# MLP of a hybrid decoder layer: one of seven products added from PSUM by VectorE in place of a ScalarE copy and a GpSimd add

## What is computed

```python
def finish_layer(x, attn_o, pool_z, ga, gp, w_attn_up, w_pool_up, w_out,
                 g_post_mix, g_pre_mlp, g_post_mlp, w_mlp_up, w_mlp_down):
...
    h = x + rms_norm(m @ w_out, g_post_mix)
    f = jnp.square(jax.nn.relu(rms_norm(h, g_pre_mlp) @ w_mlp_up)) @ w_mlp_down
    return h + rms_norm(f, g_post_mlp)
```

## Time and profile before

| | |
|---|---|
| time, median of 3 runs | 1331.14 us (1331.07 to 1332.55) |
| the profiled execution's own time | 1330.84 us |
| its span, first to last instruction | 1329.1 us |
| the 14 blocks | from about 596 to 1226 us of the span |
| busy in the span: TensorE | 1308.5 us, 98% |
| VectorE | 695.9 us, 52% |
| ScalarE | 567.4 us, 43% |
| GpSimd | 452.5 us, 34% |

### The profile page before, as it was taken

The page is one execution under the profiler, slowest core; times in us unless marked ns, Lnnn a source line. Parts: engine busy times, 40 slices in busy tenths (PEclk is TensorE's granted clock), DMA queues, the critical chain, the costliest instruction groups (busy, mean ns, idle before and its releaser), DMA issues.

```text
span 1329.1 us, 20370 instructions
## 1 busy us (share of the span) xinstructions
PE 1308.5 (98%) x7483; PEld 1205.4 (91%) x7483; DVE 695.9 (52%) x1070; ACT 567.4 (43%) x1063; POOL 452.5 (34%) x541
## 2 busy tenths in 40 slices
PE   7999999999999999999999999999999999999998
PEld 6988889999999998888989998999899989998986
DVE  6478752322222235546666566656665666566256
ACT  6355543211111144336445544554455445444432
POOL 4001584000000000103465457545754575457010
PEclk9999999999999999999999999999999999999999
DMA  8200001011111114421110111011101100110152
GB/s 256 97 33 34 17 33 38 32 48 48 48 48 34 47 57 178 146 84 60 64 64 0 63 63 55 8 63 63 46 17 63 63 35 28 63 63 32 64 189 96
DMA packets 23638, 84.42 MB, mean 64 GB/s; under 512 B 3202, under 2 KB 3282, under 8 KB 23562
## 3 DMA queue, kind: packets, MB, share of 16 engines
q1 hardware_dynamic: 17970, 64.30, 13.6%
q0 software_dynamic: 5472, 19.12, 4.4%
q10 hardware_dynamic: 144, 0.26, 0.1%
HBM read 74.38 MB, written 10.39 MB: 64 GB/s over the span
## 4 chain that ended last, share of the span: by engine, by line
PE 92%; DVE 3%; ACT 3%; issue 1%; DMA 0%; DVEq 0%; SPq 0%; ACTq 0%
PE ps L1858 20%; PE ps L1496 18%; PE ps L1497 18%; PE ps L1498 18%; PE ps L1738 9%; PE ps L1517 2%; PE ps L1891 2%; ACT pr L755 1%; DVE pr L1138 1%; PE ps L1746 1%; PE ps L1712 1%; ACT pt L775 0%; DVE pt L1185 0%; PE ps L1537 0%; PE ps L1808 0%
## 5 line engine op out<-in xcount | busy, mean ns | idle before, releaser
L1496 PE MATMUL ps<-xn,wr 128*128 128x384 f32 (+1 forms) x1384 | 455.4, 329 | 2.6 <-issue 1.5
L1497 PE MATMUL ps<-xn,wr 128*128 128x384 f32 (+1 forms) x1384 | 452.6, 327 | 0.0
L1498 PE MATMUL ps<-xn,wr 128*128 128x384 f32 (+1 forms) x1384 | 452.4, 327 | 0.0
L1496 PEld LDWEIGHTS ps<-xn,wr 128*128 128x128 f32 x1384 | 260.2, 188 | 6.7 <-issue 2.3
L1497 PEld LDWEIGHTS ps<-xn,wr 128*128 128x128 f32 x1384 | 260.3, 188 | 0.5
L1498 PEld LDWEIGHTS ps<-xn,wr 128*128 128x128 f32 x1384 | 260.1, 188 | 0.0
L618 POOL TENSOR_TENSOR acc<-acc,tmp 128x512 f32<-128x512 f32 x160 | 239.5, 1519 | 46.6 <-ACT tmp L938 44.7
L1362 DVE TENSOR_TENSOR acc<-acc,ps 128x512 f32<-128x512 f32 x216 | 143.3, 684 | 37.8 <-PE ps L1858 31.3
L938 ACT ACTIVATE tmp<-ps 128x512 f32<-128x512 f32 x168 | 97.2, 597 | 150.8 <-PE ps L1858 120.3
L1858 PE MATMUL ps<-wdh,wfh 128*128 128x512 f32 x392 | 130.3, 390 | 0.0
L1858 PE MATMUL ps<-wdl,wfh 128*128 128x512 f32 x392 | 130.1, 390 | 0.0
(11 more groups left out here) (270 smaller groups left out, 1803.6 us busy)
## 6 DMA issues: line engine op xcount, KB each, us to landing
raw<-in_weights SPq DMA_DIRECT2D x78, 512.0 KB, 3.4
wdf<-in_weights SPq DMA_DIRECT2D x28, 512.0 KB, 3.7
xrow<-in_x_prompt SPq DMA_DIRECT2D x8, 512.0 KB, 8.8
xr<-in_x_prompt POOLq DMA_DIRECT2D x8, 512.0 KB, 6.3
residual_rows<-h POOLq DMA_DIRECT2D x8, 512.0 KB, 2.9
hb<-residual_rows POOLq DMA_DIRECT2D x8, 512.0 KB, 9.7
out_y_prompt<-hb SPq DMA_DIRECT2D x7, 512.0 KB, 2.6
g<-in_vectors POOLq DMA_DIRECT2D x3, 512.0 KB, 4.5
```

The costliest lines, as they stand in the source:

```text
L1496: pe.matmul(out, wh, rh, start=(i == 0), stop=False)
L1497: pe.matmul(out, wh, rl, start=False, stop=False)
L1498: mm = pe.matmul(out, wl, rh, start=False, stop=(i == last))
```

## The change

Product 4 of each group, which belongs to the lower row tile's first column half, is no longer copied by ScalarE and added by GpSimd; VectorE adds it to `acc[:, r, 0:512]` from PSUM. Each block has eight copies and eight GpSimd adds in place of twelve, and 21 VectorE adds in place of 17. TensorE waits for VectorE where it waited for the copy: before the sample rows (for (4,0)) and before the third up group of the next block (for all of VectorE's adds).

```diff
@@ W_ADDED, W_COPIED
-    (5, 0), (5, 1), (6, 0), (3, 0), (6, 1), (3, 1), (7, 0), (7, 1), (5, 2), (5, 3), (6, 2), (3, 2), (6, 3), (3, 3),
-    (7, 2), (7, 3), "sample"])}
+    (5, 0), (5, 1), (6, 0), (3, 0), (6, 1), (3, 1), (7, 0), (7, 1), (5, 2), (4, 0), (4, 1), (5, 3), (6, 2), (3, 2),
+    (6, 3), (3, 3), (7, 2), (7, 3), "sample", (4, 2), (4, 3)])}
-    (1, 0), (1, 1), (2, 0), (2, 1), (1, 2), (4, 0), (4, 1), (1, 3), (2, 2), (2, 3), (4, 2), (4, 3)])}
+    (1, 0), (1, 1), (2, 0), (2, 1), (1, 2), (1, 3), (2, 2), (2, 3)])}
@@ GpSimd, wino_pool
                 wino_pool_add(w, (1, 2), first)
-                wino_pool_add(w, (4, 0), first)
-                wino_pool_add(w, (4, 1), first)
                 wino_pool_add(w, (1, 3), first)
                 wino_pool_add(w, (2, 2), first)
                 wino_pool_add(w, (2, 3), first)
-                wino_pool_add(w, (4, 2), first)
-                wino_pool_add(w, (4, 3), first)
@@ ScalarE, wino_from_hidden
                 wino_copy(w, (1, 2))
-                wino_copy(w, (4, 0))
-                wino_copy(w, (4, 1))
                 wino_copy(w, (1, 3))
                 wino_split(w, 1)
                 wino_copy(w, (2, 2))
                 wino_copy(w, (2, 3))
-                wino_copy(w, (4, 2))
-                wino_copy(w, (4, 3))
                 act.wait_ge(w_pool, w * N_COPY + N_COPY)
@@ VectorE, wino_add and wino_from_lows
-                a = acc[:, r, 512:]
-                if first and number in (5, 6):
+                a = acc[:, r, 0:512] if number == 4 else acc[:, r, 512:]
+                if first and number in (5, 6, 4):
...
                 wino_add(w, (5, 2), first)
                 wino_lo(w, 0)
+                wino_add(w, (4, 0), first)
+                wino_add(w, (4, 1), first)
                 wino_add(w, (5, 3), first)
...
                 wino_add(w, (7, 3), first)
                 wino_lo(w, 1)
                 wino_sample_add(w, first)
+                wino_add(w, (4, 2), first)
+                wino_add(w, (4, 3), first)
@@ TensorE, wino_up and wino_downs
                 elif i == 2:
-                    pe.wait_ge(w_copy, w * N_COPY + N_COPY)
+                    pe.wait_ge(w_add, w * N_ADD + 1)
...
-                pe.wait_ge(w_copy, copied_of(w, (4, 0)))
+                pe.wait_ge(w_add, added_of(w, (4, 0)))
                 wino_sample(w)
                 wino_pair(w, (4, 2), (4, 3))
```

More of the change, by code:

```diff
@@ L608, in wino_pool_add @@
                 number, i = m
-                r = W_ROWS[i][0] if number == 4 else W_ROWS[i][1]
+                r = W_ROWS[i][1]
                 k = W_COPIED[m]
```

## The result

The changed kernel takes 1336.23 us (median of 5 runs, 1335.28 to 1337.33) against 1331.14 us before: the ratio is 1.0037, with a 95% interval of 1.0026 to 1.0048. It is slower by about what was forecast (1335.7 us). The profiled execution took 1335.28 us, 4.44 us more than the one before; its span is 1333.5 us in place of 1329.1.

What follows compares the result with a forecast made beforehand. TensorE was taken to bound the kernel, at 44.59 us per block. Stalls of 13 x 0.31 + 0.38 and 0.14 at the end add 4.55 us to the profiled 1330.84; with 0.30 to the median, 1335.7 us, range 1332.6 to 1338.6.

Steps and rivals of the forecast that it cites:

- What is removed is worth nothing: Product 4's copies and GpSimd adds, 33 us of ScalarE and 85 us of GpSimd, lie beside TensorE's 44.59 us per block.
- The end of the block is hidden: Adds of (4,2) and (4,3) take 1.3 us of VectorE's 5.42 us wait for the next block's weights.
- One stall per block at (3,3), 0.31 us: Adds of (4,0) and (4,1) delay (5,3), so (3,3)'s weight load is 0.42 us late; 0.31 us lost per block.
- No second stall at (2,2) and (2,3): VectorE's later adds: (3,2) 0.05 us in time for (2,2), (3,3) just in time for (2,3), a further 0.04 to spare.
- Block 0 and the end: Block 0's stall costs 0.38 us; behind the last block TensorE waits 0.14 us more, for the add of (4,3).
- The sum: Whole kernel: 13 x 0.31 + 0.38 + 0.14 = 4.55 us slower, giving 1335.7 us.
- No stall: Rival: fewer GpSimd adds shorten `wino_lo` to 1.29 us or less, (5,3) is in time, 1331.3 us; chance 0.14.
- The weight load hidden: Rival: TensorE loads (3,3)'s weights while waiting, saving 0.11 us per stall; 3.0 us in all, 1334.1 us; chance 0.08.
- VectorE falls behind: Rival: (2,3) stalls too, 2.2 us more, 1337.9 us; with (2,2) as well 1340.1 us; chance 0.10.

Runs made afterwards that it cites:

- one add ahead: Changed kernel with the add of (4,1) moved behind that of (7,2), so only (4,0) stands ahead of (5,3): 1331.28 us, ratio 0.9999 to the kernel before.
- the end alone: Kernel before with only (4,2) and (4,3) moved to VectorE; (4,0) and (4,1) still copied and added by GpSimd: 1331.37 us, ratio 1.0002.
- turned banks: Up groups behind the last block take banks 1, 2, 3, 0: on one add ahead 1329.74 us, repeated 1329.97; on the kernel before 1329.66.
- the two runs that removed the first stall: Changed kernel with (5,3) added ahead of (4,0) and (4,1): 1340.18 us; or with TensorE doing all of (6,3) before (3,3): 1333.97 us.
- GpSimd kept quiet: Changed kernel with GpSimd adding only 128 of 512 columns of (2,0), (2,1) and (1,2) in the loop's 13 blocks: 1332.17 us, ratio 1.0011.

## Why the prediction was right

- **What is removed is worth nothing**: shown. With the loss out of the way (one add ahead, or the end alone) the time is that of before, to within 0.1%, and with turned banks it does not matter who adds product 4.
- **The end of the block is hidden**: shown by the end alone and by the shorter wait for the weights. Of that wait 4.1 us were expected to be left, and 4.30 were.
- **One stall per block at (3,3), 0.31 us**: the period grew by 0.31 us (44.90 against 44.59). The parts hold too: the load 0.4 us late, and 0.34 us from load to next matmul. That the load is not hidden was argued from one wait in block 0 and holds in all 14.
- **No second stall at (2,2) and (2,3)**: right, with small margins: of the 0.14 and 0.10 us between add and load the hand-over takes 0.05, which leaves 0.09 and 0.05 against 0.05 and at most 0.04 computed. In the two runs that removed the first stall both appear.
- **Block 0 and the end**: block 0 lost 0.36 us more than before, worked out as 0.38; the last wait grew by 0.17, worked out as 0.14.
- **The sum** of 4.55 us stands against 4.44 in the profiled executions and 5.1 between the medians. Added up from the trace, the twelve periods grew by 3.81 us, the last block by 0.31, block 0 by 0.36 and the last wait by 0.17, 4.65 in all; the profiled executions differ by 0.2 less, and the products of block 0 start 0.2 us earlier in the changed kernel's (623.84 against 624.04 us). The interval of the ratio, 3.5 to 6.4 us, holds all of these. The rest of the medians' difference is not settled; runs of one kernel lie 2 us apart and more.
- **No stall** was refuted as a forecast, since `wino_lo` kept its 1.71 us, for the reason given: the GpSimd adds beside it stayed. The prediction counted three of them; only (2,1) and (1,2) overlap `wino_lo`, and (2,0) overlaps `wino_low` (the rows of the last section). Its mechanism is real: with those adds cut short the stall nearly goes. That it needs `wino_lo` at 1.29 us was too strict: `wino_low` ahead of it is shortened as well, so `wino_lo` starts 0.12 us earlier in its block and is 0.24 shorter, together 0.36 of the 0.40 us that (3,3)'s load was late.
- **The weight load hidden** is refuted by 0.34 us at every stall. **VectorE falls behind** did not come about in the change; it is what the change turns into when only the first wait is taken away.

## What to carry to other kernels

An engine that is half idle over a block can still have a stretch without a gap, and work moved to it costs what it delays there; look at the timeline between the last slack and the next instruction that somebody waits for, not at the busy share. Before removing a wait of a full engine, work out the next two or three hand-overs with the stall taken out: the stall may be what keeps the rest in time. Adding from PSUM by VectorE in place of a copy and a GpSimd add was free here where each add fitted into VectorE's waiting time and the margin of its next hand-over, as in the run with one add ahead.

## What the runs showed of the hardware beyond that

VectorE's `wino_low` and `wino_lo` and GpSimd's adds lengthen each other, and by turns. In the change, one block has this `wino_low` and these three adds of GpSimd:

```profile
1171.68 1.41 DVE L1318 TENSOR_TENSOR wfl<-wff,wfh 128x896 fp32r<-128x896 f32 x1
...
1170.84 1.30 POOL L618 TENSOR_TENSOR acc<-acc,tmp 128x512 f32<-128x512 f32 x1 [2.00 <-ACT tmp L934]
1172.20 2.04 POOL L618 TENSOR_TENSOR acc<-acc,tmp 128x512 f32<-128x512 f32 x1
1174.20 2.29 POOL L618 TENSOR_TENSOR acc<-acc,tmp 128x512 f32<-128x512 f32 x1
```

The first add takes 1.30 us. The second overlaps `wino_low`, which ends at about 1173.09, and the third `wino_lo`, from 1173.61 to 1175.33. They end 1.15 and 1.16 us after these, so nearly all of an undisturbed add comes behind the VectorE instruction; the standing still is inside the row. `wino_low` is 1.41 us long there and 1.09 with GpSimd kept quiet. The Trainium skill ("SBUF — State Buffer", Who interferes with whom) calls the port pair that VectorE and GpSimd share an exclusive lock. The trace comes near that: `wino_low`, `wino_lo` and the second and third add each end 0.13 to 0.15 us sooner than if they had stood still until the other engine's row ended and then taken their undisturbed time (1.09, 1.22 and 1.30 us). Adds from PSUM, with one input in SBUF, stayed at 0.68 us throughout.

A wait of TensorE for VectorE cost about 0.11 us beyond the time by which the waiting matmul itself came late, since its weight load stood too: from the load that waited to the next matmul are 0.34 us, against 0.225 from one matmul to the next in a full stream.
